# A gated up-projection with four plain units instead of six, and the preparation matmuls moved with them

## The reference

```python
def swiglu(x, w13, w2):
    gate, up = jnp.split(x @ w13, 2, axis=-1)
    return (jax.nn.silu(gate) * up) @ w2
...
x = layer_norm(ALPHA * x + 0.5 * swiglu(x, ffn_w13[layer, 0], ffn_w2[layer, 0]), ln_g[layer, 0], ln_b[layer, 0])
```

## Time and profile before

| | us |
|---|---|
| median of 3 runs | 2161.1 |
| lowest and highest of them | 2159.67, 2168.91 |
| the profiled execution | 2159.01 |
| its span, first to last instruction | 2157.3 |
| PE busy, DVE busy, ACT busy | 2070.9 (96%), 1420.9 (66%), 866.8 (40%) |
| mean granted TensorE clock over the span | 0.982 |

### The profile page before, as it was taken

How to read it: one execution, slowest core, us unless ns; L and a number is a source line. 1 busy time by engine, 2 the same in 40 slices (tenths; PEclk the granted TensorE clock), 3 DMA queues, 4 the chain that set the end, 5 groups by cost and what they waited for, 6 DMA issues and landing times.

```text
span 2157.3 us, 43513 instructions
## 1 busy us (share of the span) xinstructions
PE 2070.9 (96%) x16575; PEld 2003.8 (93%) x16575; DVE 1420.9 (66%) x2358; ACT 866.8 (40%) x1529; POOL 228.6 (11%) x267
## 2 busy tenths in 40 slices
PE   7999999999999999999999999999978789999998
PEld 7999999999999999999999999998965589999997
DVE  4583895695894697389559835267645378838955
ACT  3351453363652354265325525222234345414533
POOL 0000002304000000400000041111012130000022
PEclk9999999999999999999999999999988899999998
DMA  4233433222233233234333323667586323323331
GB/s 144 88 116 90 131 113 101 83 69 83 87 98 96 87 97 99 74 89 152 110 95 98 110 76 115 213 206 236 162 273 209 128 74 99 101 85 98 96 95 55
DMA packets 381505, 249.87 MB, mean 116 GB/s; under 512 B 10422, under 2 KB 363038, under 8 KB 381326
## 3 DMA queue, kind: packets, MB, share of 16 engines
q1 hardware_dynamic: 371271, 210.00, 32.7%
q0 software_dynamic: 10096, 37.94, 5.1%
HBM read 230.63 MB, written 22.35 MB: 117 GB/s over the span
## 4 chain that ended last, share of the span: by engine, by line
PE 76%; DVE 11%; DMA 4%; issue 4%; ACT 3%; SPq 1%; POOL 1%; DVEq 0%; ACTq 0%; POOLq 0%
PE pair L795 32%; PE pair L927 31%; PE pair L834 5%; DMA t_w_raw<-in_attn_w_kv 3%; PE pair L1075 2%; PE pair L1324 1%; DVE t_w_seven L2044 1%; DVE t_w_sum L2039 1%; PE pair L807 1%; DVE t_w_lo L1922 1%; DVE t_u_sum L2327 1%; DMA t_w_raw<-in_ffn_w 1%; ACT t_w_hi L1456 1%; DVE t_x_diff_lo L2016 1%; DVE t_stream L2252 1%
## 5 line engine op out<-in xcount | busy, mean ns | idle before, releaser
L927 PE MATMUL pair<-t_x_diff_hi,t_w_seven 128*128 128x272 f32 x1960 | 409.9, 289 | 0.0
L1456 ACT ACTIVATE t_w_hi<-t_w_raw 128x1024 fp32r<-128x1024 f32 (+2 forms) x140 | 163.8, 1172 | 412.3 <-PE pair L795 342.9
L1922 DVE TENSOR_TENSOR t_w_lo<-t_w_raw,t_w_hi 128x1024 fp32r<-128x1024 f32 (+2 forms) x140 | 216.7, 1548 | 160.0 <-ACT t_w_hi L1456 154.5
L927 PEld LDWEIGHTS pair<-t_x_diff_hi,t_w_seven 128*128 128x128 f32 x1960 | 320.3, 188 | 0.0
L927 PE MATMUL pair<-t_x_hi,t_w_seven 128*128 128x272 f32 x1120 | 240.0, 294 | 5.3 <-DVE t_c L2048 3.9
L927 PE MATMUL pair<-t_x_diff_lo,t_w_seven 128*128 128x272 f32 x840 | 241.7, 288 | 0.0
L795 PE MATMUL pair<-t_h_lo,t_w_hi 128*128 128x272 f32 x1144 | 236.5, 288 | 0.0
L795 PE MATMUL pair<-t_h_hi,t_w_lo 128*128 128x272 f32 x1144 | 236.5, 288 | 0.0
L795 PE MATMUL pair<-t_h_hi,t_w_hi 128*128 128x272 f32 x1144 | 236.3, 288 | 0.0
L927 PEld LDWEIGHTS pair<-t_x_hi,t_w_seven 128*128 128x128 f32 x1120 | 184.5, 188 | 15.8 <-issue 11.8
L795 PEld LDWEIGHTS pair<-t_h_hi,t_w_lo 128*128 128x128 f32 x1144 | 179.4, 188 | 0.0
(11 more groups left out here) (333 smaller groups left out, 5203.1 us busy)
## 6 DMA issues: line engine op xcount, KB each, us to landing
t_w_raw<-in_ffn_w SPq DMA_DIRECT2D x280, 256.0 KB, 3.1
t_w_raw<-in_ffn_w SPq DMA_DIRECT2D x64, 704.0 KB, 4.6
t_w_raw<-in_ffn_w SPq DMA_DIRECT2D x36, 512.0 KB, 3.7
t_cached<-in_cache_kv_w POOLq DMA_DIRECT2D x16, 1024.0 KB, 8.7
t_cached_v<-in_cache_kv_w POOLq DMA_DIRECT2D x16, 1024.0 KB, 10.9
t_w_raw<-in_attn_w_kv SPq DMA_DIRECT2D x24, 512.0 KB, 7.7
t_w_raw<-in_attn_w_q SPq DMA_DIRECT2D x12, 512.0 KB, 4.1
scratch_bias_rows<-scratch_bias_row SPq DMA_DIRECT2D x12, 384.0 KB
```

Source lines behind the costliest of these rows:

```text
L927: m = nc.tensor.matmul(out[:, 0:HALF], w[:, k, :], b, start=start and k == 0 and j == 0, stop=k == 3 and j == 2, skip_group_check=not start)
L1456: nc.scalar.activation(whi[s][:, 0:KT[stage], :], raw[s][:, 0:KT[stage], :], ACT.Copy) \
L1922: nc.vector.tensor_tensor(lo[:, 0:k, :], raw[s][:, 0:k, :], hi[:, 0:k, :].bitcast(F32), ALU.subtract).then_inc(lo_made[s], 1)
```

## The change

`PLAIN["up0a"]` goes from 6 to 4, so units 4 and 5 are made with seven products. The preparation moves one place forward: `start_params` stands after unit 0, `start_tables` after unit 1, and the six terms of the samples' bias no longer stand in a row after unit 3 but one ahead of each of the first six blocks of unit 2's gate product. ACT and DVE take the samples' bias out after `hidden_hi` and `hidden_lo` of unit 2, the last but one plain unit. DVE makes the differences of x after unit 0 instead of after unit 2, with a wait for the state's transposes. SP loads two units whole less and two units in quarters more, and stores the tables ahead of unit 3's weights instead of ahead of unit 5's.

```diff
-PLAIN = {"up0a": 6, "up1a": 4, "up2a": 4, "up3a": 4, "up0b": 0, "up1b": 0, "up2b": 0, "up3b": 0}
+PLAIN = {"up0a": 4, "up1a": 4, "up2a": 4, "up3a": 4, "up0b": 0, "up1b": 0, "up2b": 0, "up3b": 0}
...
-            for i in range(1, 5):
+            for i in range(1, 3):
                 stream("up0a", i)
             sp.wait_ge(tab_evac, NG)
             sp.dma_start(tab_one.ap(), tab[:]).then_inc(tab_stored, 16)
-            stream("up0a", 5)
+            stream("up0a", 3)
             sp.wait_ge(tab_stored, 16)
             for i in range(PLAIN["up0a"], KH):
                 stream_seven("up0a", i)
-                bias_piece(0 if i < 10 else 1, (i - 6) % 4)
+                if i >= 6:
+                    bias_piece(0 if i < 10 else 1, (i - 6) % 4)
...
-            def start_samp_bias():
-
-                pe.wait_ge(tab_evac, NG)
-                for v in range(6):
-                    for half, cols in enumerate((slice(0, NG * P), slice(NG * P, NG * (P + BW)))):
-                        m = nc.tensor.matmul(pc[:, half, 0:cols.stop - cols.start], rb_s[:, v, :], oh_s[:, v, cols],
-                                             start=v == 0, stop=v == 5)
-                m.then_inc(sb_mm, 1)
+            def samp_bias(v):
+
+                if v == 0:
+                    pe.wait_ge(tab_evac, NG)
+                if v > 5:
+                    return
+                for half, cols in enumerate((slice(0, NG * P), slice(NG * P, NG * (P + BW)))):
+                    m = nc.tensor.matmul(pc[:, half, 0:cols.stop - cols.start], rb_s[:, v, :], oh_s[:, v, cols],
+                                         start=v == 0, stop=v == 5)
+                if v == 5:
+                    m.then_inc(sb_mm, 1)
...
-                    products(gate_out, 0, DC, stream_x, stream_xl, own=weights(stage, 0, i)).then_inc(w_used[0], 1)
+                    products(gate_out, 0, DC, stream_x, stream_xl, each=each, own=weights(stage, 0, i)).then_inc(w_used[0], 1)
...
                     turn(0)
-                    for i in range(1, PLAIN[stage]):
-                        turn(i)
-                        if i < 4:
-                            (start_params, start_tables, start_samp_bias)[i - 1]()
+                    start_params()
+                    turn(1)
+                    start_tables()
+                    turn(2, samp_bias)
+                    turn(3)
...
                         if stage in NORMED:
                             add_shift(stage, 1)
+                        else:
+                            start_samp_bias()
                         continue
...
-                    if f == 0 and 1 <= i < 4:
-                        (start_params, start_tables, start_samp_bias)[i - 1]()
+                    if f == 0:
+                        (start_params, start_tables)[i]()
...
                         hidden_lo(stage, i)
+                        if f == 0:
+                            start_samp_bias()
                         continue
...
-                    if f == 0 and i == 3:
-                        start_samp_bias()
                     if i == n - 4:
+                        if f == 0:
+                            dve.wait_ge(st_t, 1)
                         for m in (1, 3) if f else (0, 2, 1, 3):
                             x_diff(f, m)
```

More of the change, by code:

```diff
@@ L990, in up, with turn @@
                 base, gated, hidden = USED[stage], GATED[stage], HIDDEN[stage]
-                def turn(i):
+                def turn(i, each=None):
                     gate_out, up_out = (pc, pd) if aside(stage, i) else (pa, pb)
```

## The result

The changed kernel takes 2173.5 us (median of 9 runs, 2172.15 to 2174.65), the kernel before 2159.2 (2157.64 to 2168.91): a ratio of 1.0058 with a 95% interval of 1.0046 to 1.0070. The forecast was 2173, slower by a little over what can be told from no change. In the profiled pair the span grew from 2157.3 to 2171.8 us.

The account below looks back on a forecast made before the run. PE, almost without a pause in the first stage, and its granted clock were taken as the bound. Terms of -2.3 - 3.1 + 1.4 + 1.6 + 3.05 + 9.8 + 1.3 = +11.8 us on 2161.1 gave 2173; own range 2169 to 2177, overall 2160 to 2177.

Parts of the forecast that it names:

- first wait: Ahead of unit 2's first term, PE idles until ACT has copied the tables: 1.4 us more.
- A: Rival: the clock holds through unit 2, so the sum is +2.0, 2163.1 us; chance 0.20.
- B: Rival: the clock falls at the first wait but returns after one short stretch, +3.6, 2164.7 us; chance 0.10.
- C: Rival: ACT or DVE are ready early, the waits don't show, the clock holds: -3.8, 2157.3 us; chance 0.04.
- Two units: In the first stage, two plain units become seven-products, 10.87 instead of 12.03 us each: 2.3 us less.
- The half-clock stretch of before: The slow clock in and behind the kernel before's run of six terms goes: 3.1 us less.
- Changes of kind: Between fp32r and fp32 on PE, six trips instead of two at 0.4 us each: 1.6 us more.
- Second wait: Ahead of unit 3, PE idles until DVE has added the mask to the samples' sum: 3.05 us more.
- The clock through unit 2: Half clock for five terms, the gate's blocks between them and 24 matmuls behind: 9.8 us more, bounds 0 and 13.
- A second fall: Behind the idle PE ahead of unit 3, another 3.4 us at half clock: 1.3 us more, bounds 0 and 1.5.
- DVE as the limit: If DVE holds the two new seven-products to 12.03 us, their gain is 0 and the forecast 2175.4 us.
- the row from 1425 to 1438.5 us: Counter-evidence: there fp32r products alternate with small matmuls of another kind and the clock stays at 1.00.

Follow-up runs that it names:

- e5: Changed kernel with PE's wait for the tables' copies kept ahead of unit 2's gate product, but the terms in its up product: 2163.7 us, ratio 1.0002.
- e10: Kernel before with its six terms two by two ahead of blocks 0, 2 and 4 of unit 3's up product: 2158.6 against 2160.5 us.
- e8: The changed kernel run again without any edit, with a second profile: 2172.8 against 2163.1 us, ratio 1.0048.
- e2: Changed kernel with the terms thinner and later, ahead of blocks 4 and 6 of unit 2's gate product and 0, 2, 4, 6 of its up product: 2159.2 us.
- e4: Changed kernel with the terms ahead of the first six blocks of unit 2's up product instead of its gate product: 2163.7 us, ratio 1.0014.
- e6: Changed kernel with the tables half a unit sooner, ahead of unit 1's up product, so PE does not pause before the terms: 2163.3 us, ratio 1.0005.
- e9: Changed kernel with its pause and first term kept, but two blocks between terms instead of one: 2165.3 us, ratio 1.0016.
- e3: Changed kernel with DVE's samples' sum ahead of unit 2's `hidden` and ACT's copy ahead of `hidden_hi`: 2167.4 us, ratio 1.0038.
- e12: Changed kernel with terms paired in unit 2's up product, samples' bias taken out sooner, and PE's `up0a` seven-product loop written out: 2158.8 against 2163.0 us.

## Why the prediction was right, and where it fell short

The mechanism came out as forecast, for the reason given: at unit 2 the clock fell behind the first wait and the terms kept it down (A and B of the rivals are out, C too, since both waits are there). The first term, which the prediction counted into the time without fp32r work, is not needed for the fall (e5). That the time came out to half a microsecond is luck, as is shown behind the terms. Term by term:

- Two units, -2.3: from the first seven-product to `up0b`'s first, before 227.38 - 107.25 = 120.13 and after 239.03 - 97.18 = 141.85; the two more take 10.86 each, so -2.3. DVE does not limit them.
- The half-clock stretch of before, -3.1: e10 gives -2.35 with two trips more, -3.15 without.
- First wait, +1.4: PE idles 1.40, and the first term starts 1.5 us later than the matmul behind the tables did in the kernel before (51.80 - 48.30 against 2.02).
- Changes of kind, 0.4 a trip: 2.04 us for a term and its block less 0.88 and 0.75 (six times 0.125) is 0.41.
- Second wait, +3.05: 2.73 of idle time, 2.9 from start to start (the next matmul was due at 82.16). DVE's `hidden` began 0.4 us behind that instant where I had read 0.65 at the end of unit 4.
- The clock through unit 2, +9.8: the largest term and slightly too small. The first term with its block takes 54.70 - 51.80 = 2.90 us and loses 0.9, the five others lose 3.71 - 2.04 = 1.67 each, 8.4 us, and the 15 matmuls that follow at half clock 1.5 more: some 10.7. What I left out is that the trips too take longer at half clock, 1.67 - 0.88 - 6 x 0.10 = 0.2 each (a term takes 56.75 - 54.70 = 2.05 us up to its block, where 1.8 was forecast), and the loss in the first term's trip; the clock came back a little sooner than I had counted.
- A second fall, +1.3: it did not come in the first profile and came in e8. In the seven profiles with a wait of 2.5 us or more at this place (the changed kernel, e2, e4, e5, e6, e8, e9) it came six times.

Without the second fall these make -2.3 - 3.1 + 1.5 + 1.6 + 2.9 + 10.7 = 11.3, against 11.9 measured in the first stage, of which 0.4 lies ahead of the tables. What the prediction had not at all is `up1a`: it took the change to end with its stage, and PE's wait there grew by 1.3 us with a half-clock stretch in some runs. On the median two misses cancel: the difference measured is 14.3 us where 11.8 were forecast, and the median that these were added to, 2161.1 of three runs, is 2159.2 with nine. In the sum itself a second fall that did not come (1.3) stands in for part of `up1a` and of the clock. The forecast's own range is also a little wider than the terms it names give (2170 to 2176), and with DVE as the limit the sum is 2175.2; nothing hangs on either.

What speaks in the prediction against the forecast, the row from 1425 to 1438.5 us, was no mistake: e4 and e6 show that it holds at unit 2 as well, as long as there is no pause. The Trainium skill's rule on matmul groups parted by short pauses (TensorE: Matmul & The Clock Gate, "A second HAM failure mode: psum-queue depth-cycling") names pauses, and the runs agree in that the alternation alone did nothing; what they show beyond it is one pause, and a clock that then stays at the lower level instead of swinging.

## What to carry to other kernels

Count a wait on TensorE twice where light matmuls (few rows, float32) stand beside it: once as idle time, and once as the clock that it brings down and that they then do not let return. Light matmuls go where dense work lies ahead of them and between them, a few at a time, with what they wait for done long before and with their results taken out ahead of the next long piece of work in the other engine's queue. And when a program changes its length, look for transfers in later stages that have become late: a code load may have moved into them.

## What the runs showed of the hardware

- A pause of 1.4 us between 2 us of float32 matmuls with 33 rows and the next work brought the granted clock from 1.00 to 0.50 in all five profiles that have it (the changed kernel, e3, e5, e8, e9); the same tables with fp32r work right behind them left it at 1.00 in the nine others, and a pause of 1.51 us between fp32r matmuls in all fourteen.
- How long it then stays there depends on the work: 3.4, 6.8 or 23.9 us with no term, one for two blocks, one for each block, though PE is busy without a gap in all three (the first two in one profile each).
- A load of program code (16 KB, about 1 us) in the midst of a transfer of 256 KB went with a wait of DVE of 1.2 to 1.7 us for that transfer in all eleven profiles that have it. The Trainium skill (Runtime: NRT & Kernel Launch, "Instruction fetch mechanics") says that an engine fetches its program in such blocks over a DMA queue and that this is mostly hidden. Here it is not hidden from DVE, which waits; with the load elsewhere (e12) it does not. That the code load shares one of the DMA engines with the quarter is what fits, but no run showed it directly.
